# A hybrid attention block: one output step moved to head 0, and three tiles' selection masks combined and written by GpSimd

## The reference

```python
logits = jnp.einsum('bqhd,bsd->bqhs', qib, ki32)
idx_score = jnp.einsum('bqhs,bqh->bqs', jax.nn.relu(logits), wib)
idx_score = jnp.where(admissible[None], idx_score, NEG)
_, sel = lax.top_k(idx_score, topk)            # 256, ties to the lower key
scores = scores - slopes[None, :, None, None] * dist[:, None]
p = jax.nn.softmax(jnp.where(valid[:, None], scores, NEG), axis=-1)
...
mixed = jnp.concatenate([oa * jax.nn.silu(a_z), ob * jax.nn.silu(b_z)], axis=-1)
x = x + jnp.einsum('bse,ed->bsd', mixed, w_out[l])
```

## Time and profile before

| | |
|---|---|
| median of 3 executions | 558.63 us (558.44 to 558.78) |
| profiled execution, its own time | 558.53 us |
| its span (first to last instruction) | 556.7 us |
| TensorE busy | 544.2 us (98%) |
| VectorE busy | 444.9 us (80%) |
| ScalarE busy | 372.4 us (67%) |
| GpSimd busy | 185.6 us (33%) |
| granted TensorE clock, mean | 0.999 |

### The profile page before, as it was taken

How to read it: one execution, slowest core, us unless ns; L and a number is a source line. 1 busy time by engine, 2 the same in 40 slices (tenths; PEclk the granted TensorE clock), 3 DMA queues, 4 the chain that set the end, 5 groups by cost and what they waited for, 6 DMA issues and landing times.

```text
span 556.7 us, 8938 instructions
## 1 busy us (share of the span) xinstructions
PE 544.2 (98%) x2968; PEld 461.7 (83%) x2968; DVE 444.9 (80%) x1111; ACT 372.4 (67%) x713; POOL 185.6 (33%) x285
## 2 busy tenths in 40 slices
PE   8999999999999999999999999999999999999997
PEld 7998888888888888878888888778787888889886
DVE  5786878899989999999879888887778878876631
ACT  5985777759986777768987577865555556565510
POOL 1871000104369995765220003730203030020230
PEclk9999999999999999999999999999999999999999
DMA  8724100004321111212212245311211102021032
GB/s 249 235 69 133 38 20 21 0 22 128 101 75 55 38 39 42 92 39 58 57 40 75 86 124 174 111 57 59 82 32 56 59 19 77 1 61 35 2 114 75
DMA packets 39982, 39.69 MB, mean 71 GB/s; under 512 B 6144, under 2 KB 28160, under 8 KB 39936
## 3 DMA queue, kind: packets, MB, share of 16 engines
q1 hardware_dynamic: 38416, 39.11, 23.5%
q10 hardware_dynamic: 1520, 0.01, 0.2%
HBM read 30.72 MB, written 8.39 MB: 70 GB/s over the span
## 4 chain that ended last, share of the span: by engine, by line
PE 81%; DVE 13%; ACT 3%; issue 2%; POOL 0%; ACTq 0%; POOLq 0%; DVEq 0%
PE ps_proj L1107 42%; PE ps_proj L1287 11%; PE ps_lg L1135 5%; PE ps_lg L1134 5%; PE ps_tp L1244 5%; PE ps_proj L1259 4%; PE ps_lg L1287 3%; DVE cand L1538 2%; DVE xT_lo L1769 2%; PE ps_tp L1206 1%; PE ps_lg L1082 1%; DVE lo_f L1759 1%; PE ps_tp L1280 1%; DVE w_lo L1443 1%; ACT xT_hi L999 1%
## 5 line engine op out<-in xcount | busy, mean ns | idle before, releaser
L1107 PE MATMUL ps_proj<-w_hi,xT_hi 128*128 128x512 f32 (+1 forms) x432 | 165.0, 382 | 1.5 <-DVE xT_lo L1398 1.1
L1107 PE MATMUL ps_proj<-w_lo,xT_hi 128*128 128x512 f32 (+1 forms) x432 | 161.1, 373 | 0.0
L1107 PE MATMUL ps_proj<-w_hi,xT_lo 128*128 128x512 f32 (+1 forms) x432 | 161.0, 373 | 0.0
L942 ACT ACTIVATE ps_lg<-score,cand 128x768 f32<-128x768 f32 (+2 forms) x96 | 96.0, 1000 | 10.6 <-DVE cand L1538 10.3
L1107 PEld LDWEIGHTS ps_proj<-w_lo,xT_hi 128*128 128x128 f32 x432 | 81.4, 188 | 14.9
L1107 PEld LDWEIGHTS ps_proj<-w_hi,xT_hi 128*128 128x128 f32 x432 | 81.4, 189 | 14.5 <-DVE xT_lo L1398 2.0
L1107 PEld LDWEIGHTS ps_proj<-w_hi,xT_lo 128*128 128x128 f32 x432 | 81.6, 189 | 11.9
L999 ACT CAST xT_hi<-ps_tp 128x128 fp32r<-128x128 f32 (+3 forms) x89 | 40.4, 488 | 61.8 <-PE ps_tp L1244 61.2
L1769 DVE TENSOR_TENSOR xT_lo<-ps_tp,xT_hi 128x128 fp32r<-128x128 f32 (+3 forms) x89 | 47.0, 558 | 30.0 <-ACT xT_hi L999 29.9
L983 ACT ACTIVATE lo_f<-lo_f,negmax 128x128 f32<-128x128 f32 (+7 forms) x64 | 50.2, 785 | 0.2
L1443 DVE SCALAR_TENSOR_TENSOR w_lo<-stage,g_in,w_hi 128x512 fp32r<-128x512 f32 x48 | 44.3, 926 | 7.3 <-ACT w_hi L794 6.8
(11 more groups left out here) (195 smaller groups left out, 1141.8 us busy)
## 6 DMA issues: line engine op xcount, KB each, us to landing
stage<-in_w_in_dram SPq DMA_DIRECT2D x48, 256.0 KB, 2.6
x_in<-in_x_dram SPq DMA_DIRECT2D x8, 512.0 KB, 4.7
lo_f<-in_x_dram SPq DMA_DIRECT2D x7, 512.0 KB, 4.0
out_dram<-lo_f SPq DMA_DIRECT2D x7, 512.0 KB, 3.5
q_scratch<-nat SPq DMA_DIRECT2D x8, 256.0 KB, 2.0
q_in<-q_scratch SPq DMA_DIRECT2D x8, 256.0 KB, 3.8
stage<-in_w_out_dram SPq DMA_DIRECT2D x8, 256.0 KB, 2.6
z_scratch<-nat SPq DMA_DIRECT2D x8, 256.0 KB, 2.1
```

The costliest lines, as they stand in the source:

```text
L942: act.activation(ps_lg[i % 2][:, 0:keys(t)], score[:, sc_off[t]:sc_off[t] + keys(t)], ACT.Sign, bias=cand[:, t:t + 1].bitcast(F32), scale= ...
L1107: mm = pe.matmul(ps_proj[u % 2][:, 0:n], a[:, k, rows], b[:, k, 0:n], start=(k == 0 and i == 0), stop=(k == KB - 1 and i == 2))
```

## The change

- **Mask.** For tiles 5, 6 and 7 `select` ends with the ties kept, written into `rank`. GpSimd's new `mask(t)` adds `gt`, makes 0 or -1e30 of the sum and adds the negative distances: three instructions over `keys(t)` columns, each waiting for the one before. `mask(5)` stands behind `finish_b(1)`, `mask(6)` behind `finish_b(3)`, and `mask(7)` between `finish_b(5)` and `finish_b(6)`. `gt` becomes 16 bits wide. The late steps are fewer (25 for 31) and `LATE_AT` places them anew.
- **Step at head 0.** From tile 4 on one output step is run at head 0, ahead of `mT`, and head 5 of tiles 3 to 6 runs two in place of three.
- **Tile 7's z** is finished at m = 16 in place of 15, and the first output step waits for one unit less.
- **Tile 4's rows** in `ps_lg` begin at column 128, so that its 640 columns are cut 384 + 256 in place of 512 + 128 (`dot_keys`), for the indexer as for the scores.
- **Sums.** `y_sums(2)` runs at head 3 of tile 3 in place of head 5.

```diff
--- before.py
+++ after.py
@@ -197,7 +197,7 @@
         wT_sgu = place("wT_sgu", [P, G, P], F32)
         q_in = [place("q_in0", [P, B_W], F32, at=zone_k), place("q_in1", [P, B_W], F32, at=top[0])]
         vg_row = place("vg_row", [P, A_W], F32)
-        gt = place("gt", [P, S], I8)
+        gt = place("gt", [P, S], F16)
         eq = place("eq", [P, S], I8)
         x_sq = place("x_sq", [P, S], BF16, at=top[0])
         rank = place("rank", [P, S], F16)
@@ -314,6 +314,8 @@
         q_step = sem("q_step")
         q_normed = sem("q_normed")
         mask_ready = sem("mask_ready")
+        ties_kept = sem("ties_kept")
+        mask_step = sem("mask_step")
         q_loaded = [sem(f"q_loaded{i}") for i in range(2)]
         z_loaded = [sem(f"z_loaded{i}") for i in range(2)]
         res_loaded = sem("res_loaded")
@@ -394,7 +396,8 @@
         for m in range(len(STEPS_BZ)):
             for n in range(sum(STEPS_BZ[:m]), sum(STEPS_BZ[:m + 1])):
                 if n % KB == KB - 1:
-                    last_units[m] = FREE + n // KB
+                    last_units[m + (n == KB * (T - FREE) - 1)] = FREE + n // KB
+        assert (UNITS - 1) % 2 == 1
         FIRST_HALF_W_AT = {2: FREE, 5: FREE + 1, 9: FREE + 2, 13: FREE + 3}
         W_AT = (16, 16, 17, 17, 18, 21, 21, 22)
         BY_POOL = 5
@@ -410,6 +413,14 @@
         def x_blocks(t):
 
             return (slice(0, 4), slice(4, KB)) if t < IN_HALVES else (slice(0, KB),)
+
+        def row_at(t):
+
+            return P if t == 4 else 0
+
+        def lg_row(m, t):
+
+            return ps_lg[m % 2][:, row_at(t):row_at(t) + keys(t)]
 
         def head_no(t, h):
             return H * t + h
@@ -753,11 +764,28 @@
                 pool.wait_ge(last_w_scaled, k + 1)
                 pool.tensor_tensor(lo, raw, hi.bitcast(F32), ALU.subtract).then_inc(w_lo_done, 1)
 
+            def mask(t):
+
+                n, i = keys(t), t - SPLIT
+                row = score[:, sc_off[t]:sc_off[t] + n]
+                pool.wait_ge(ties_kept, i + 1)
+                pool.tensor_tensor(rank[:, 0:n], rank[:, 0:n], gt[:, 0:n], ALU.add).then_inc(mask_step, 1)
+                pool.wait_ge(mask_step, 2 * i + 1)
+                pool.tensor_scalar(row, rank[:, 0:n], -1.0, -NEG, ALU.add, ALU.mult).then_inc(mask_step, 1)
+                pool.wait_ge(mask_step, 2 * i + 2)
+                pool.tensor_tensor(row, row, negdist[:, S - n:S], ALU.add).then_inc(mask_ready, 1)
+
             finish_b(0)
             for k in range(BY_POOL):
                 last_w(k)
             for t in range(1, T):
+                if t == T - 2:
+                    mask(T - 1)
                 finish_b(t)
+                if t == 1:
+                    mask(SPLIT)
+                if t == 3:
+                    mask(SPLIT + 1)
 
 
         @block.scalar
@@ -907,7 +935,7 @@
                     act.wait_ge(logits_done, m + 1)
                     if m >= 2:
                         act.wait_ge(score_acc, m - 1)
-                    act.activation(relu_sb[:, m % 2, 0:keys(t)], ps_lg[m % 2][:, 0:keys(t)],
+                    act.activation(relu_sb[:, m % 2, 0:keys(t)], lg_row(m, t),
                                    ACT.Relu).then_inc(relu_done, 1)
 
             for t in range(T0, T):
@@ -1128,11 +1156,13 @@
                 pe.wait_ge(proj_evac, unit(IQ, t) + 1)
                 four_pairs(tp(("qi", t)), nat[:, unit(IQ, t) % 2, :]).then_inc(qiT_done, 1)
 
-            def dot_keys(bank, stack, h, hh, ll, n):
-                for a in range(0, n, BANK):
-                    b = min(n, a + BANK)
-                    pe.matmul(bank[:, a:b], stack[:, h, :], hh[:, a:b], start=True, stop=False)
-                    mm = pe.matmul(bank[:, a:b], stack[:, h, :], ll[:, a:b], start=False, stop=True)
+            def dot_keys(m, stack, t, h, hh, ll):
+
+                row, cut = lg_row(m, t), BANK - row_at(t)
+                for a, b in ((0, min(cut, keys(t))), (cut, keys(t))):
+                    if a < b:
+                        pe.matmul(row[:, a:b], stack[:, h, :], hh[:, a:b], start=True, stop=False)
+                        mm = pe.matmul(row[:, a:b], stack[:, h, :], ll[:, a:b], start=False, stop=True)
                 return mm
 
             def logit(t, h):
@@ -1143,7 +1173,7 @@
                 pe.wait_ge(qi_lo_done, 2 * (t - T0) + h % 2 + 1)
                 if m >= 2:
                     pe.wait_ge(relu_done, m - 1)
-                dot_keys(ps_lg[m % 2], qi_stack[t % 2], h, ki_hh, ki_ll, keys(t)).then_inc(logits_done, 1)
+                dot_keys(m, qi_stack[t % 2], t, h, ki_hh, ki_ll).then_inc(logits_done, 1)
 
             def index(t):
 
@@ -1233,7 +1263,7 @@
                     pe.wait_ge(max_done, m - 1)
                 if m == 4 * H:
                     pe.wait_ge(*tp_release(third_users[-1]))
-                dot_keys(ps_lg[m % 2], q_stack[t % 2], h, k_hh, k_ll, keys(t)).then_inc(s_done, 1)
+                dot_keys(m, q_stack[t % 2], t, h, k_hh, k_ll).then_inc(s_done, 1)
 
             def pT(t, h):
                 m = head_no(t, h)
@@ -1301,7 +1331,7 @@
                         if t == 0:
                             pe.wait_ge(w_lo_done, KB * (O1 + n) + k + 1)
                             if n == 0 and k == 0:
-                                pe.wait_ge(proj_evac, UNITS)
+                                pe.wait_ge(proj_evac, UNITS - 1)
                         mm = out_block(t, n, k)
                         if k == KB - 1:
                             mm.then_inc(out_acc, 1)
@@ -1328,10 +1358,10 @@
                 if t == 2:
                     return 2
                 if h == 0:
-                    return 2 if t == 3 else 0
-                return 3 if h == 7 or h == 5 and t < T - 1 else 2
-
-            steps_left = 2 * KB - sum(steps_at(T - 1, h) for h in range(H))
+                    return 2 if t == 3 else 1
+                return 3 if h == 7 else 2
+
+            steps_left = 2 * KB - sum(steps_at(T - 1, h) for h in range(1, H))
             pending = last_projections()
             for t in range(T):
                 for h in range(H):
@@ -1597,8 +1627,12 @@
                     then(dve.tensor_tensor_scan(rank[:, cut:n], eq[:, cut:n], eq[:, cut:n], rank[:, cut - 1:cut],
                                                 ALU.add, ALU.max))
                     yield
-                then(dve.scalar_tensor_tensor(out=eq[:, 0:n], in0=rank[:, 0:n], scalar=room[:, t:t + 1],
-                                              in1=eq[:, 0:n], op0=ALU.is_le, op1=ALU.mult))
+                kept = dve.scalar_tensor_tensor(out=(rank if t >= SPLIT else eq)[:, 0:n], in0=rank[:, 0:n], scalar=room[:, t:t + 1],
+                                                in1=eq[:, 0:n], op0=ALU.is_le, op1=ALU.mult)
+                if t >= SPLIT:
+                    kept.then_inc(ties_kept, 1)
+                    return
+                then(kept)
                 yield
                 then(dve.scalar_tensor_tensor(out=gt[:, 0:n], in0=gt[:, 0:n], scalar=-1.0, in1=eq[:, 0:n],
                                               op0=ALU.add, op1=ALU.add))
@@ -1731,7 +1765,7 @@
 
             late = late_steps()
 
-            LATE_AT = ((2, 4, 6), (0, 1), (1, 2, 7), (1, 2, 5, 6), (1, 2, 5, 6), (0, 1, 2, 5, 6), (1, 2, 3, 5), ())
+            LATE_AT = ((2, 4, 6, 7), (0, 1), (1, 2, 7), (5, 6), (1, 2, 5), (1, 2, 5, 6), (1,), ())
 
 
             def twice_silu(t):
@@ -1756,7 +1790,7 @@
                         dve.wait_ge(mask_ready, t - T0 + 1)
                     d = score[:, sc_off[t]:sc_off[t] + keys(t)]
                 blocks = lambda v: v.rearrange("p (b s) -> p b s", s=P)
-                dve.tensor_tensor_reduce(probs[m % 2][:, 0:t + 1, :], blocks(ps_lg[m % 2][:, 0:keys(t)]), blocks(d),
+                dve.tensor_tensor_reduce(probs[m % 2][:, 0:t + 1, :], blocks(lg_row(m, t)), blocks(d),
                                          -(2.0 ** -(h + 1)), BIG, ALU.add, ALU.min,
                                          negmax[:, t % 2, h:h + 1]).then_inc(max_done, 1)
 
@@ -1842,7 +1876,7 @@
                         twice_silu(last_units[m])
                     if m in FIRST_HALF_W_AT:
                         lo_w(KB * O1 + FIRST_HALF_W_AT[m])
-                    if h == (3 if t < 3 else 5) and t > 0:
+                    if h == (3 if t < 4 else 5) and t > 0:
                         y_sums(t - 1)
                     if m in W_AT[BY_POOL:]:
                         if m == W_AT[BY_POOL]:
```

## The result

The changed kernel takes 559.79 us in the median (559.48 to 560.74), the kernel before 558.63 (558.44 to 558.78): ratio 1.0023, interval [1.0015, 1.0031], so 1.16 us slower; each is the median of twelve executions. Forecast were 559.9, in a range of 556.6 to 562.3. The profiled execution, with 559.48 us the shortest of its twelve, has a span of 557.7 us, 1.0 more than before. One execution each of the later kernels `e1`, `e3`, `e5` and `e7` took 904 to 1,918 us and is left out of the ratios, and in `e5` and `e7` it is the profiled one, so that their traces say nothing of single stalls.

The account below looks back on a forecast made before the run. TensorE is busy for 98% of the span, so time changes only where it stands still. Gains -3.8, new wait +3.9 and clock +1.2 make +1.3 us: 558.53 + 1.3 + 0.1 = 559.9 us, range 556.6 to 562.3.

Parts of the forecast that it names:

- output step at head 0: Turns into tiles 4 to 6: the step fills TensorE's stalls before mT, 0.69, 0.69 and 0.60, together 2.0 us gained.
- twice_silu one head later: Tile 7's silu and tanh no longer delay the mixes that the first output step waits 0.79 us for: 0.6 us gained.
- tile 4's columns: Tile 4's index and score heads: cutting 384 + 256 columns saves TensorE 0.05 us in each of 16 heads, say 0.7 us.
- masks off VectorE: Tile 6, head 4: a mask instruction no longer stands before lo_q, so TensorE's stall goes, 0.8 us gained.
- allowance for slow scans: Tile 5's scans move to heads 1 and 2 of tile 2, where GpSimd works on the last weights: 0.3 us lost.
- new stall: Turn into tile 7: VectorE waits for mask(7) on GpSimd, so mT(5, 0) starts 3.9 us later; TensorE idles 4.2 us.
- clock: The 4.2 us idle stretch of TensorE in tile 7 lets the granted clock fall, costing 1.2 us, bounds 0 and 2.4.
- Rival A: The clock stays up, all else as forecast: 558.7 us, no change; chance 0.22.
- Rival B: The mask is fast on GpSimd (3.8 us), TensorE idles 1.8 and the clock holds: 556.3 us; chance 0.15 with Rival E.
- Rival D: GpSimd is slower, 9.3 us for the mask: +3.1, 563.0 us; chance 0.08.
- Rival C: Gains come in by half, as stalls filled at head 0 reopen at heads 5 and 6: 561.8 us; chance 0.15.
- Rival E: Masks were hidden, so their move does nothing; only step, silu and cut count: -3.3, 555.3 us; chance 0.15 with Rival B.

Follow-up runs that it names:

- e1: Changed kernel with mask(7) placed ahead of finish_b(5) on GpSimd instead of behind it: 554.43 us, ratio 0.9924 to the kernel before.
- e3: Changed kernel with the masks of tiles 5 to 7 back on VectorE and late steps where they were before, the rest kept: 554.84 us, ratio 0.9933.
- e5: e1 with the output step of head 0 put back into head 5: 556.54 us, ratio 0.9964 to the kernel before.
- e7: e1 with tile 4's rows back at column 0, so 512 + 128 columns: 555.33 us, ratio 0.9942 to the kernel before.
- e6: e1 with tile 7's tanh and silu back at m = 15 and the first output step waiting for all units: 554.99 us, ratio 0.9937.
- e4: Changed kernel with 28 idle transposes keeping TensorE busy ahead of mT(5, 0) in tile 7: 558.55 us, ratio 1.0000 to the kernel before.
- e9: Changed kernel with one memset more on VectorE, of a tile nothing reads, after the last y_sums: 558.66 us, ratio 1.0002 to the kernel before.
- e2: Changed kernel with y_sums(5) at head 3 of tile 6 instead of head 5, mask(7) still behind finish_b(5): 554.58 us, ratio 0.9928.
- e8: e1 with four late steps moved, so none is left at head 5 of tiles 4 and 5: 552.19 us, ratio 0.9888 to the kernel before.

## Why the prediction was right, step by step

| step | forecast, us | measured, us | from |
|---|---|---|---|
| output step at head 0 | -2.0 | -2.1 | `e5` |
| twice_silu one head later | -0.6 | -0.56 | `e6` |
| tile 4's columns | -0.7 | -0.9 | `e7` |
| masks off VectorE | -0.8 | -1.3 | `e3` against `e1`, to `bias_max(7, 0)` |
| allowance for slow scans | +0.3 | (in the line above) | |
| sum of the gains | -3.8 | -4.85 | 493.15, now 488.30 |
| new stall | +3.9 | +3.5 | 3.80 less the 0.31 of before |
| clock | +1.2 | +1.2 | `e4` |
| last store | none | +1.1 | `e9` |
| all | +1.3 | +1.0 | span, the lines above sum to 0.95; +1.16 by medians |

The mechanism was right in each link: `mask(7)` behind `finish_b(5)` behind `y_sums(5)`, one wait of VectorE for GpSimd (forecast 5.6 us, measured 5.6), TensorE idle for close to 4 us (forecast 4.2, measured 3.80), the clock down after it. `e1`, `e2` and `e4` take out one link each and get back about what it was said to cost. The stalls at the turns into tiles 5 and 6 and at (6, 4) went, as forecast. Rival A fell, since the clock did fall; `e4` shows what it would have been, 558.55 (forecast 558.7). Rival B fell too: the mask took 5.5 us, nearer to 6.2 than to 3.8. Each two-input instruction is 2.14 or 2.12 us, forecast 2.4, because I drew the line from 8 columns through the slower of two rows of 512 columns in the earlier trace rows, 1.28 us; through the other, 1.04, it would have given 1.9. The masks of 768 and 896 columns took 1.66 and 1.90. 16-bit inputs are no faster than 32-bit ones. The Trainium skill ("GPSIMD Engine Reference", Elementwise — side-by-side cycle accounting) has 4,497 ns for 2,048 columns, and by an estimate from it each would take 2.25; that comes closer, and the trace agrees with it within 6%. Rival D's slow GpSimd isn't seen. Rival C has its mechanism and not its size: the uneven spacing at (5, 6) grew from 0.36 us before to 0.65, which `e8` removes, but that at (4, 6) fell from 0.54 to 0.42, and both lie within the gains above. Rival E's ground, that the masks' move is worth nothing, is refuted by the 1.3 us of `e3` against `e1`.

That the number was met so closely is in part luck: the gains were 1.05 us larger than forecast and the stall 0.4 smaller, and a loss of 1.1 that the prediction doesn't have made up for most of it.

The term that was mis-sized is the sum of the gains, 3.8 for 4.85. Half of the difference are the masks, which I priced by one stall at (6, 4) ("It goes, and 1.22 covers the whole 0.8 us"). They had stood in front of other slots as well: at (6, 6) two transposes started 0.40 us apart in the kernel before and 0.41 in `e3`, and 0.11 in the changed kernel. The allowance for slow scans was hardly needed (tile 5's two scans of 384 columns take 1.51 and 1.12 us now, 1.79 and 1.01 before). The columns have a slip in the sum: 0.64 less 0.58 is 0.06 and not 0.05, and 16 times that is 0.96, close to the 0.9 measured. What `gt` in 16 bits was said to cost, nothing, holds: the sum less one over 1,024 columns takes 1.22 us with 8-bit values (L1603 before) and with 16-bit ones (`e3`).

The stall was 0.4 too large, since the mask took 0.7 us less than forecast and `finish_b(5)` had come 0.3 later than the gains would have it. The missing term is the last store, +1.1: the prediction ends with the last instruction that computes. With the gains right and the store left out, the forecast would have been 558.53 - 4.85 + 3.9 + 1.2 + 0.1 = 558.9 and no change; `e9` measures that kernel at 558.66. So the change, by all that it does to the order of work, is worth nothing, and its 0.2% loss is where its instruction count happens to end.

## What to carry to other kernels

When work is moved to an engine with time to spare, look at what it queues behind, not at its load: GpSimd was 36% busy, and one mask placed one step too late took back all but 0.16 us of a gain of 4.85, while the same mask one place earlier left it whole. A stall of TensorE can cost its own length and then the clock: 3.8 us idle cost 1.2 more. And when two kernels differ by a microsecond, compare the times of the last compute and of the last store's landing before a cause is sought in the order of work.

## What was not expected of the hardware

One instruction more in VectorE's list moved a kernel of 559 us by 1.1 us: with 1,344 the last fetch of instructions (8 KB in queue 14) fell into the last store, which took 3.1 to 3.2 us from issue to landing for 256 KB, and 2.0 without it. The clock fell 5.0 us after the end of TensorE's last product, at 493.30, when it had already worked again since 492.10; at the end of the kernel before it fell 2.5 us into the idle time. GpSimd's two-input instruction over 1,024 columns takes 2.14 us with 16-bit inputs and output and 2.12 with 32-bit ones.
